# First up projection by Strassen in two groups of F tiles, with the modulation weights moved beside the down projections

## The reference, cut to what matters

```python
mod = (silu(c) @ w_ada + b_ada)            # 9 sections of 1024: shift, scale, gate for each of three blocks
h = modulate(rms_norm(x, g1), mod[0], mod[1])
x = x + 0.5 * mod[2] * ((silu(h @ Wg1) * (h @ Wu1)) @ Wout1)      # FFN 1, 2816 hidden
h = modulate(rms_norm(x, gmix), mod[3], mod[4])
x = x + mod[5] * (concat(pool_mixer(h @ Wa), gmlp_mixer(h @ Wzb)) @ Wmix_out)
h = modulate(rms_norm(x, g2), mod[6], mod[7])
x = x + 0.5 * mod[8] * ((silu(h @ Wg2) * (h @ Wu2)) @ Wout2)      # FFN 2, 2816 hidden
out = rms_norm(x, gfin)
```

## Time and profile before

| | |
|---|---|
| median of 3 runs | 884.86 us (884.81 to 887.31) |
| the profiled execution's own time | 886.71 us |
| its span in the profile | 885.0 us |
| TensorE busy | 859.1 us (97%) |
| VectorE busy | 584.4 us (66%) |
| ScalarE busy | 332.3 us (38%) |
| chain that ended last | PE 90%, DVE 5%, ACT 2% |
| mean granted clock of TensorE | 0.991 |
| moved by DMA | 134.46 MB, mean 152 GB/s |

### The profile page before, as it was taken

How to read it: one execution, slowest core, us unless ns; L and a number is a source line. 1 busy time by engine, 2 the same in 40 slices (tenths; PEclk the granted TensorE clock), 3 DMA queues, 4 the chain that set the end, 5 groups by cost and what they waited for, 6 DMA issues and landing times.

```text
span 885.0 us, 13666 instructions
## 1 busy us (share of the span) xinstructions
PE 859.1 (97%) x5290; PEld 743.5 (84%) x5290; DVE 584.4 (66%) x902; ACT 332.3 (38%) x434; POOL 36.0 (4%) x42
## 2 busy tenths in 40 slices
PE   4999999999999999999999999999999999999996
PEld 3778888888888888897887898899988899999886
DVE  4579777777776756538645469988633588885443
ACT  6232222222223221225424346665521256664323
POOL 0000000000000000000340000000000000100000
PEclk9899999999999999999999999999999999999998
DMA  9977666666656555434533322566343576562322
GB/s 268 289 215 234 191 191 191 192 194 191 194 179 204 160 172 166 146 108 108 142 96 96 94 73 72 139 173 171 85 130 93 118 181 165 148 168 83 99 66 96
DMA packets 219501, 134.46 MB, mean 152 GB/s; under 512 B 5577, under 2 KB 214589, under 8 KB 219453
## 3 DMA queue, kind: packets, MB, share of 16 engines
q1 hardware_dynamic: 216516, 128.52, 50.1%
q0 software_dynamic: 2880, 5.24, 3.7%
q10 hardware_dynamic: 56, 0.01, 0.0%
HBM read 126.41 MB, written 2.10 MB: 145 GB/s over the span
## 4 chain that ended last, share of the span: by engine, by line
PE 90%; DVE 5%; ACT 2%; SPq 1%; DMA 1%; issue 1%; ACTq 0%
PE ps L1569 22%; PE ps L1571 21%; PE ps L1570 21%; PE ps L1948 7%; PE ps L1944 7%; PE ps L1946 7%; PE ps L1826 1%; PE ps L1760 1%; DMA ada_first<-in_w_ada_dram 1%; PE ps L1827 1%; PE ps L1828 1%; DVE h_lo L1021 1%; DVE sw_lo_a L1447 1%; SPq L397 1%; DVE xs L1014 0%
## 5 line engine op out<-in xcount | busy, mean ns | idle before, releaser
L1569 PE MATMUL ps<-h_hi,w_split 128*128 128x512 f32 (+1 forms) x464 | 179.8, 388 | 5.5 <-DVE h_lo L1021 5.3
L1571 PE MATMUL ps<-h_hi,w_split 128*128 128x512 f32 (+1 forms) x464 | 180.0, 388 | 0.0
L1570 PE MATMUL ps<-h_lo,w_split 128*128 128x512 f32 (+1 forms) x464 | 178.9, 386 | 0.0
L968 DVE TENSOR_TENSOR w_split<-w_raw,w_split 128x2048 fp32r<-128x2048 f32 (+1 forms) x45 | 93.3, 2073 | 75.9 <-ACT w_split L610 75.9
L1569 PEld LDWEIGHTS ps<-h_hi,w_split 128*128 128x128 f32 x464 | 87.4, 188 | 26.9 <-issue 4.5
L610 ACT CAST w_split<-w_raw 128x2048 fp32r<-128x2048 f32 (+1 forms) x45 | 77.1, 1714 | 81.8 <-PE ps L1571 72.7
L1570 PEld LDWEIGHTS ps<-h_lo,w_split 128*128 128x128 f32 x464 | 87.6, 189 | 18.4
L1571 PEld LDWEIGHTS ps<-h_hi,w_split 128*128 128x128 f32 x464 | 87.6, 189 | 16.6
L1065 DVE SCALAR_TENSOR_TENSOR ada_acc<-ada_raw,c_act,ada_acc 128x256 f32<-128x256 f32 x196 | 95.1, 485 | 7.0
L1944 PE MATMUL ps<-sums_hi,sw_hi 128*128 128x256 f32 x320 | 89.3, 279 | 0.9 <-DVE sw_lo_a L1447 0.5
L1946 PE MATMUL ps<-sums_lo,sw_hi 128*128 128x256 f32 x320 | 89.6, 280 | 0.0
(11 more groups left out here) (186 smaller groups left out, 1533.2 us busy)
## 6 DMA issues: line engine op xcount, KB each, us to landing
ada_raw<-in_w_ada_dram SPq DMA_DIRECT2D x56, 512.0 KB, 3.6
sw_raw<-in_ffn_w_in_dram SPq DMA_DIRECT2D x100, 256.0 KB, 4.1
w_raw<-in_ffn_w_in_dram SPq DMA_DIRECT2D x47, 512.0 KB, 6.0
ada_first<-in_w_ada_dram SPq DMA_DIRECT2D x16, 512.0 KB, 7.4
w_raw<-in_ffn_w_out_dram SPq DMA_DIRECT2D x16, 384.0 KB, 4.0
w_raw<-in_w_mix_in_dram SPq DMA_DIRECT2D x12, 512.0 KB, 4.3
sw_raw<-in_ffn_w_out_dram SPq DMA_DIRECT2D x16, 384.0 KB, 4.1
w_raw<-in_ffn_w_out_dram SPq DMA_DIRECT2D x16, 320.0 KB, 3.3
```

The lines of the kernel that those rows point to most:

```text
L968: nc.vector.tensor_tensor(w_lo[s][:, 0:n], w_raw[s][:, 0:n], w_hi[s][:, 0:n].bitcast(F32), ALU.subtract).then_inc(lo_ready, 1)
L1569: nc.tensor.matmul(dst, w_h, a_h, start=start, stop=False)
L1570: nc.tensor.matmul(dst, w_h, a_l, start=False, stop=False)
L1571: return nc.tensor.matmul(dst, w_l, a_h, start=False, stop=stop)
```

## The change

FFN 1 takes the form of FFN 2. All helpers of FFN 2 get an index f and serve both.

- The first 8 tiles of F stay plain steps (`PLAIN = (8, 2)`), 14 go by Strassen: 3 in the first group of 11, then `down2(0, 0, m)` for 8 tiles m, then 11 more, then `down2(0, 1, m)`. a_hi and a_lo go; b_hi and b_lo serve both FFNs. The down products add to x in two parts, with the gate negated.
- The activation sums of FFN 1 are made beside the plain steps 2 and 3.
- The modulation unit is 512 columns wide, 14 units of two halves (four blocks of D, 1 MB each). A half is four multiply-adds of 512 elements; the second half of a unit also does the transpose and the sum. Eight halves run beside plain steps 0, 1, 1, 2, 4, 4, 5, 5 through ada_raw, which now holds one half; six beside each of FFN 1's two down groups and four beside the first down group of FFN 2 ("hosted": their data lie in the free end of the sw_raw slot of the down weights); four beside the mix.
- The modulation columns are taken over from the sums in five portions (`take_mod`, `TAKES`) in place of two.
- The mix's v weights have a buffer of their own (v_raw) and are requested within FFN 1's second down group.
- The order of SP's list, of VectorE's and of ScalarE's changes accordingly.

SP's list, the new part:

```diff
+            for j in range(2, PLAIN[0]):
+                load_pair(ffn1_w_in, j, j % 2, UP1 + j)
+                for part in {2: (0,), 3: (1, 2), 4: (3,), 5: (4,), 6: (5, 6), 7: (7,)}.get(j, ()):
+                    load_ada(part)
+            sp.wait_ge(ada_link, used(7))
+            for n in range(N0[0]):
+                load_up(0, n)
+            for m in range(KD):
+                load_down2(0, 0, m)
+            for n in range(N0[0], NS[0]):
+                load_up(0, n)
+            for m in range(KD):
+                load_down2(0, 1, m)
+                if m == KD - 4:
+                    sp.wait_ge(sw_used[0], pieces(0, up_item(0, NS[0] - 1) + 1))
+                    for kq in range(2):
+                        load_v(w_mix_in, kq)
+            sp.wait_ge(sw_lo_ready[0], pieces(0, down_item(0, 1, KD - 1) + 1))
+            sp.wait_ge(ada_link, used(19))
             for q in range(2):
+                load_two(w_mix_in, q * UNIT // 2, q, MIXIN + 2 + q)
+            load_ada(20)
+            sp.wait_ge(last_done, 2)
             sp.dma_start(ws_raw[:], w_spatial[0].rearrange("h t s -> t h s")).then_inc(ws_full, 16)
...
+            load_ada(21)
             for q in range(2, 4):
+                load_two(w_mix_in, q * UNIT // 2, q % 2, MIXIN + 2 + q)
             for q in range(KD // 2):
+                load_two(w_mix_out, q * UNIT // 2, q % 2, MIXOUT + q)
+                if q >= 2:
+                    load_ada(20 + q)
```

The two loaders of modulation halves:

```diff
+            def load_ada(part):
+                n = ADA_RAW.index(part)
                 for s in range(2):
+                    if n:
+                        sp.wait_ge(ada_link, used(ADA_RAW[n - 1], (s + 1) * KA // 2))
+                    k0 = part % 2 * KA + s * KA // 2
+                    sp.dma_start(ada_raw[:, s], w_ada_v[:, k0:k0 + KA // 2, ada_cols(part)])\
+                      .then_inc(ada_full[s], 16)
+            def load_down2(f, g, m):
+                i = down_item(f, g, m)
+                s = i % 2
+                sw_free(f, i, False)
...
+                if i in HOSTED[f]:
+                    part = HOSTED[f][i]
+                    k0 = part % 2 * KA
+                    host_free(f, i)
+                    sp.dma_start(host_view(s), w_ada_v[:, k0:k0 + KA, ada_cols(part)]).then_inc(host_full[f][s], 16)
```

VectorE and ScalarE beside FFN 1's plain steps:

```diff
+    ADA_PLAIN = {0: (0,), 1: (1, 2), 2: (3,), 4: (4, 5), 5: (6, 7)}
...
+            for j in range(PLAIN[0]):            # VectorE
+                plain_product(0, j)
+                if j == 0:
+                    for part in range(2):
+                        split_lo_part(2, part)
+                elif j + 2 < PLAIN[0]:
+                    split_lo(j + 2)
+                if j == 3:
+                    hsum_2(0)
+                    hsum_4(0)
+                    hsum_rest(0, 2)
+                    hsum_rest(0, 3)
+                plain_lo(0, j)
+                for part in ADA_PLAIN.get(j, ()):
+                    ada_own(part)
+                if j == 2:
+                    shift_difference(0)
+                    hsum_1(0)
+                    hsum_3(0)
+                    hsum_rest(0, 0)
+                    hsum_rest(0, 1)
+                elif j == PLAIN[0] - 2:
+                    add_blocks(0, 0)
+                    rest_up(0, 0, 0)
+                    rest_up(0, 0, 1)
+                elif j == PLAIN[0] - 1:
+                    rest_up(0, 0, 2)
+            up_group(0, 0)
...
+            for j in range(PLAIN[0]):            # ScalarE
+                plain_silu(0, j)
+                if j == 0:
+                    split_hi_part(2, 0)
+                    split_hi_part(2, 1)
+                elif j + 2 < PLAIN[0]:
+                    split_hi(j + 2)
+                if j == 2:
+                    plain_hi(0, j)
+                if j in (2, 3):
+                    for r in (2 * j - 4, 2 * j - 3):
+                        hsum_split(0, r)
+                if j != 2:
+                    plain_hi(0, j)
+                if j == PLAIN[0] - 2:
+                    for c in range(3):
+                        cast_up(0, 0, c)
+            first_group(0)
```

VectorE beside the down groups of FFN 1, and TensorE's list there:

```diff
+            for m in range(KD - 1):
...
+                rest_down(0, 1, m + 1)
...
+                if down_item(0, 1, m) in HOSTED[0]:
+                    ada_hosted(0, down_item(0, 1, m))
+                update_last(0, m)
+                add_squares(X_AT[0] + m + 1)
...
+            pe.wait_ge(prod_ready, 1)
+            plain(0, 2)
+            for j in range(3, PLAIN[0]):
+                pe.wait_ge(prod_ready, j - 1)
+                pair(j % 2, UP1 + j, (2 * (j % 2), 2 * (j % 2) + 1), h_hi, h_lo)
+            for n in range(N0[0]):
+                strassen(0, n)
+            sum_units(0)
+            for m in range(KD):
+                down2(0, 0, m)
+            for n in range(N0[0], NS[0]):
+                strassen(0, n)
+            for m in range(KD - 1):
+                if m == KD - 2:
+                    sum_units(1)
+                down2(0, 1, m)
```

More of the change, by code:

```diff
@@ L742, in copy_out @@
                 nc.scalar.copy(out_tok[:, :, bass.ds(m * P, P)], src).then_inc(out_copied, 1)
-            def down(base, x_count, sq_count, last):
-                nc.scalar.activation(dummy, ones[:, 0:1], ACT.Sqrt)
-                with act.Fori(0, KD - 1) as m:
-                    for s in range(2):
-                        split_hi(s, HALF, (m * 2 + (base + s + 2), m + (base // 2 + 1)))
-                    square(m, m + x_count, m + (sq_count + 1))
-                    if last:
-                        copy_out(m)
-                if not last:
-                    split_hi(0, FULL, base + 2 * KD)
-                act.wait_ge(sq_added, sq_count + KD)
@@ L761, in _ @@
+            first_group(0)
+            for n in range(N0[0], NS[0]):
+                up_slot(0, n)
+            for m in range(KD - 1):
+                cast_down(0, 1, m + 1)
+                if m == 0:
+                    product_hi(0, NS[0] - 1)
+                    nc.scalar.activation(dummy, ones[:, 0:1], ACT.Sqrt)
+                square(m, 0)
+            split_hi(MIXIN)
+            act.wait_ge(sq_added, KD)
             square_half(KD - 1, 0, 1, 0)
@@ L952, in _ @@
+            hsum_split(1, 0)
+            for c in range(3):
+                cast_up(1, 0, c)
+            hsum_split(1, 1)
+            hsum_split(1, 2)
+            plain_hi(1, 0)
+            plain_silu(1, 1)
+            first_group(1)
+            for n in range(N0[1], NS[1]):
+                up_slot(1, n)
+            for m in range(KD - 1):
+                cast_down(1, 1, m + 1)
+                if m == 0:
+                    product_hi(1, NS[1] - 1)
                     nc.scalar.activation(dummy, ones[:, 0:1], ACT.Sqrt)
-                square2(m)
+                square(m, 2)
@@ L1537, in _ @@
-            for n in range(N0):
-                up_slot(n)
+            split_lo_part(UP2 + 1, 0)
+            hsum_1(1)
+            split_lo_part(UP2 + 1, 1)
+            add_blocks(1, 0)
+            plain_product(1, 0)
+            hsum_rest(1, 0)
+            rest_up(1, 0, 0)
+            hsum_3(1)
+            hsum_2(1)
+            rest_up(1, 0, 1)
+            hsum_rest(1, 2)
+            hsum_rest(1, 1)
+            hsum_4(1)
+            rest_up(1, 0, 2)
+            plain_lo(1, 0)
+            hsum_rest(1, 3)
@@ new lines, in down2_half @@
+            def down2_half(m, half, between=None):
+                cols = HALVES[half]
+                hi, lo = (v.rearrange("p (k n) -> p k n", n=P) for v in (down_hi(m), down_lo(m)))
+                for k in range(GF):
+                    if between:
+                        between(k)
+                    ins = product(ps[:, LAST_BANK[half], cols], hi[:, k, :], lo[:, k, :], b_hi[:, k, cols],
+                                  b_lo[:, k, cols], k == 0, k == GF - 1)
+                ins.then_inc(last_done, 1)
@@ L2021, in _, with units_beside @@
-            for n in range(N0):
-                strassen(n)
+            pe.wait_ge(prod_ready, P_AT[1])
+            plain(1, 1)
+            def units_beside(k, n):
+                if k == GF // 2 + 1:
+                    pe.wait_ge(root_ready, 5)
+                    sum_units(n)
+            for n in range(N0[1]):
+                strassen(1, n)
             for m in range(KD):
-                down2(0, m)
-            for n in range(N0, NS):
-                strassen(n)
+                down2(1, 0, m, (lambda k, m=m: units_beside(k, 3 + m // 2)) if m in (1, 3) else None)
```

1352 lines of the change are left out of this document (606 added, 746 removed).

## The result

The changed kernel takes 909.84 us (median of 4 runs, 907.6 to 913.36), the kernel before on the same chip 884.84: a ratio of 1.028, 95% interval 1.0242 to 1.0318. So it is 25 us slower, where 20.8 were forecast (905.5 us, range 892 to 914). The profiled execution took 910.12 us, with a span of 908.4.

What follows compares the result with a forecast made beforehand. TensorE was taken to bound the kernel, VectorE next and full in the plain steps. FFN 1 saves 15.3 us and loses 30.4 (+15.1); mix +0.8, FFN 2 +1.4, clock +3.5: +20.8 on 884.86, forecast 905.5 us, range 892 to 914.

Steps and rivals of the forecast that it cites:

- the changes between up and down: Three switches between FFN 1's up and down parts: TensorE waits, 2.9 us including one short wait for the last chunk's weights.
- step 4: FFN 1 plain step: pair 4, requested behind parts 1 and 2, is split late, so the step starts 0.9 us late.
- step 5: FFN 1 plain step: VectorE's part 3 and activation sums delay the split, so the step starts 2.6 us late.
- step 7: FFN 1 plain step: pair 7 stands behind requests for parts 5 and 6, so the step starts 8.1 us late.
- first Strassen product: FFN 1 after step 7: its loads wait for all of part 7, so it starts 7.8 us late.
- third half product: First Strassen tile of FFN 1: late accumulation data delay VectorE and then ScalarE's copy, a 2.2 us wait.
- sixth chunk: FFN 1's second down group: chunk 5's weights land behind a hosted request and the v loads, 5.9 us late.
- sum of units 12: FFN 2: `sum_units(3)` needs parts 24 and 25 in one slot before block 6 of the second chunk, +1.4 us.
- the clock: After the 8.1, 7.8 and 5.9 us waits in FFN 1, TensorE's granted clock falls: +3.5 us.
- The clock staying up: Rival 1: no clock falls, since the waits lie in a dense stretch; +17.3 us, 902 us, chance 0.23.
- A queue slower or faster throughout: Rivals 2 and 3: DMA at 0.9 of the rate, 910 to 914 us, or 1.15 times, 897 to 900; chance 0.13 each.
- Rival 4: Plain steps: SP's list doesn't hold up the pairs, pair 7 requested by 103 us; 879.5 us, or 873; chance 0.08.

Runs made afterwards that it cites:

- e10: e8 with the v weights requested later, w_spatial ahead of half 20, and the sum of units 12 one block later: 875.27 us, ratio 0.988 to the kernel before.
- e8: Changed kernel with three buffers for the halves and the first Strassen tile requested early, pairs and halves in the change's own order: 880.62 us, ratio 0.9933.
- e9: e6 plus later v loads, earlier w_spatial, later sum of units 12, and three extra VectorE operations in each of plain steps 2 to 6: span 883.8 us.
- e4: Changed kernel with unused matmuls filling TensorE's waits at steps 4 and 7 and the first and third half products: 908.58 us, ratio 1.025.
- e1: Changed kernel with each pair of w_ffn1 requested ahead of the modulation halves it stood behind: 899.73 us, ratio 1.0142 to the kernel before.
- e3: Changed kernel with halves 0 to 7 in their own buffer, first Strassen loads not waiting for part 7: span from step 2's start 4.6 us shorter.
- e2: Changed kernel with the multiply-adds of the eight plain-step halves cut to 32 columns instead of 512: span 901.9 us, single execution.
- e6: Changed kernel with three buffers for the halves, the first Strassen tile requested early, and pairs ahead of halves as in e1: 881.9 us, ratio 0.9949.

## Why the prediction was right

**What is saved.** The period of a Strassen tile in FFN 1's second group, from VectorE's timeline, is 9.79 us (forecast 9.90):

```profile
263.30 0.69 DVE L1250 TENSOR_TENSOR ev<-ps,ev 128x512 f32<-128x512 f32 x1 [0.53 <-PE ps L1791]
273.09 0.69 DVE L1250 TENSOR_TENSOR ev<-ps,ev 128x512 f32<-128x512 f32 x1 [0.53 <-PE ps L1791]
```

That is not a better tile. In the traces the tiles have one of two periods, 9.89 or 9.79 us, one for a whole group at a time, and the kernel before has both: 9.89 in FFN 2's first group (the rows at 590.10 and 600.00 that I took in the earlier trace rows) and 9.79 in its second (721.28, 731.06, 740.85). The changed kernel has 9.79 in FFN 1's second group and 9.89 in FFN 2's second, e10 9.79 in both. A group of 11 tiles differs by 1.0 us between the two, which is more than several of the terms of the prediction; what sets the period was not found.

With the waits gone (e10) the first v product comes 13.0 us earlier than before (331.3 against 344.3). By my terms it would be 15.3 less 2.9 for the changes between up and down: 12.4. So the saving was there, as the earlier trace rows had it.

**VectorE's prices.** They held to the hundredth: multiply-add 0.751 us, transpose 0.712 (taken: 0.71), sum 0.686 (0.69), by the groups:

```profile
L1095 DVE SCALAR_TENSOR_TENSOR work<-ada_raw,c_act,work 128x512 f32<-128x512 f32 x42 | 31.5, 751 | 9.8 <-DMA ada_raw<-in_w_ada_dram 8.6
L1100 DVE STREAM_TRANSPOSE work<-work 128x512 f32<-128x512 f32 x14 | 10.0, 712 | 0.5
L1102 DVE TENSOR_REDUCE ada_part<-work 128x16 f32<-128x512 f32 x14 | 9.6, 686 | 0.5
```

The 66 us of work in the plain stretch were right too (63.2 busy in e8, and e9 shows that there is no room).

**The waits, term by term.** Forecast, then measured: step 4 0.9 and 3.4; step 5 2.6 and 1.0; step 7 8.1 and 8.8; first Strassen product 7.8 and 7.8; third half product 2.2 and 2.6; sixth chunk 5.9 and 2.8; w_spatial 0.8 and 0.9; sum of units 12 1.4 and 1.1; the three changes between up and down and the last chunk's weights 2.9 and 1.8 (0.4, 0.5, 0.7 and 0.2). The waits stand where they were forecast, and both large ones were right within 0.7 us: pair 7 came 7.4 us after its request (taken: 7.2), the first tile's loads 7.0 (6.8). Step 7 is right as a difference: pair 7 was requested 2.4 us later than forecast, and the step was due later too. Three terms were mis-sized.

Step 4: the cast came 10.0 us after the pair's request in place of 7.3. The queue wasn't slow, it carried 297 GB/s between the two. But it moved 4.1 MB from 60 us to the cast, and parts 1 and 2 and pair 4 are 3.1 MB:

```profile
60.00:77.75 17.75, 17.75 (x79) 14.55 (x79) 11.88 (x16) 1.22 (x2) 0.00 (x0) 1.00 0.80 233
```

So it was already carrying what was requested behind pair 4, and my assumption that requests are served one by one in the order of issue does not hold here. Step 5: 1.6 us less than forecast, since step 4's late start and its fall of the clock had put off the time at which it was due.

The sixth chunk: the prediction's own rate was not followed in its sum. 3.8 MB at 265 to 285 GB/s take 13.3 to 14.3 us and not the 15.9 from 371.6 to 387.5; by that rate the wait would have been 3.3 to 4.3 us. Measured, hosted half, v weights and chunk weights, 3.9 MB, landed 13.0 us after the first request:

```profile
378.10 0.37 SPq L523 DMA_DIRECT2D sw_raw<-in_w_ada_dram  x1
378.51 2.36 SPq L439 DMA_DIRECT2D v_raw<-in_w_mix_in_dram  x4
380.91 2.06 SPq L517 DMA_DIRECT2D sw_raw<-in_ffn_w_out_dram  x2
...
391.15 1.37 ACT L794 CAST sw_hi<-sw_raw 128x1408 fp32r<-128x1408 f32 x1 [3.02 <-DMA sw_raw<-in_ffn_w_out_dram]
```

Up to the second down group the changed kernel is 30.6 us behind e8 (296.9 against 266.3). Five waits are 23.6 of that. The four stretches at half speed make some 6: products of 512 columns start 0.43 us apart in place of 0.23 (127.57, 127.99, 128.42), for 2.9 to 3.4 us each. My terms for this part were 21.6 of waits and at most 3.5 for the clock, 5.5 short. The v loads, sized too large, gave 3.1 of it back, and behind FFN 2's second Strassen tile 1.0 more was lost than forecast, as much as the longer period there costs: so 25 came out and not 20.8. That the total is so near is in part luck, since the errors have both signs. (884.86 and 20.8 are 905.7; the 905.5 on record is a slip of 0.2.) Keeping the clock up (e4) gives 3.9 of the 6 us back; which wait takes up the rest was not tried singly.

**The clock.** Three falls were forecast, four came in FFN 1: after the waits of 3.4, 8.8 and 7.8 us, and after the 2.6 that followed shortly on the third. The wait of 2.8 before the sixth chunk brought none; I had counted one there. By the Trainium skill (TensorE: Matmul & The Clock Gate, "What's actually happening") the half rate is the default and an idle stretch brings it back: the trace agrees, at 0.50 in the window from 124 to 127 us. My 3.5 us stood for falls after the first Strassen product's wait and the sixth chunk's; the second did not come, and those that came cost some 6 where they stood.

**The rivals.** The clock staying up (902) is refuted by the windows. A queue slower or faster throughout is not borne out: the landings behind the two long waits took 7.4 and 7.0 us, near the 7.2 and 6.8 taken, while step 4's came later than forecast and the sixth chunk's earlier. Rival 4, the other side, was to be decided by whether pair 7 goes out by 103 or at 112.8. It went out at 115.2. In e8 it goes out at 94.9, the steps start in time, and the ratio of 0.9933 puts the median at 878.9, where rival 4 had 879.5; with the rest hidden it had 873, and e10's 0.988 gives 874. So rival 4 named the right switch. Its price is right by luck: its sum leaves out the sixth chunk (2.9 us in e8) and counts 4.8 for step 5 and the third half product, which don't wait in e8. As for the cause, the prediction had both parts of it, the one buffer and the order of the list; e1, e8 and e10 weigh them. The order matters only as long as one buffer holds one half, so that each request waits for VectorE.

## What to carry to other kernels

When an engine's list mixes loads for a bound engine (pairs for TensorE) with loads for a busy helper (halves for VectorE), every wait of the second kind is a wait of the first kind: look for the single buffer that makes a request wait for its consumer, and give it a second place in memory that is free at that time, before reordering the list (here the order alone gave 11 us from the common start, buffers and the first tile's early request 30). When a change saves on the bound engine and slows the kernel, take marks relative to a common start: here they put nearly all the loss into 100 us at the beginning, and the saving, untouched, behind it. An engine with 63 us of work in 66 is not yet a bottleneck, but only if nothing in its inputs has a round trip through its own progress.

## What the runs showed of the hardware

- A 3.4 us wait of TensorE at step 4, between dense stretches, was followed by a fall of the granted clock (0.65 over 81 to 85 us), and so was one of 2.48 us (e3). One of 2.78 us was not (1.00 over 394 to 398), nor one of 3.00 (e2, 1.00 over 387 to 391), while one of 2.97 (e6, 0.50 over 366 to 370) and one of 3.03 (e4, 0.52 over 391 to 394) were. Between 2.5 and 3.0 us the length of the wait alone does not tell whether the clock falls.
- Products that nobody reads kept the clock at 2.4 GHz through waits of 3 to 8 us in the plain steps (1.00 over 57 to 390 us of e4) and brought the first down group up to 3.9 us forward; the intervals of the two kernels' ratios overlap (1.0233 to 1.0267 and 1.0242 to 1.0318).
- The queue carried 338 GB/s over 6 us (388 to 394) and 353 over 4 us in e6, above the 285 of the earlier trace rows. Where the v loads came, it carried more: 401 over 4 us (381 to 385). The Trainium skill (DMA: Bandwidth & Descriptors, "Where 436 GB/s comes from") has some 358 GB/s as the limit of a core's share of the memory; the window at 381, in a program that runs on one core, is above it.
- The queue did not carry requests one at a time: when pair 4 was cast, 4.1 MB had moved since 60 us, 1 MB more than pair 4 and all requested ahead of it.
- A Strassen tile took 9.79 or 9.89 us, the same for a whole group, and the same code had one in one execution and the other in another (FFN 2's second group: 9.79 before, 9.89 in the changed kernel, 9.79 in e10).
- The same VectorE operation of 512 elements took 0.418 us into SBUF and 0.685 into PSUM (e9, the groups below). The Trainium skill (VectorE: DVE Perf Modes, "Why PSUM operands drop a tier") has it that an operand in PSUM takes away the fast mode that such an operation has in SBUF; the two rows agree. Here the operand in PSUM is the one that is written.

```profile
381.00:385.00 4.00, 4.00 (x19) 3.30 (x18) 3.89 (x5) 0.00 (x0) 0.00 (x0) 1.00 1.05 401
388.00:394.00 6.00, 3.46 (x16) 2.50 (x14) 2.14 (x2) 1.50 (x2) 0.00 (x0) 1.00 1.12 338
...
81.00:85.00 4.00, 2.87 (x7) 2.32 (x8) 3.89 (x6) 0.00 (x0) 0.00 (x0) 0.65 0.23 58
```

```profile
L1428 DVE TENSOR_SCALAR ps<-h_lo 128x512 f32<-128x512 f32 x10 | 6.4, 685 | 0.0
...
L1428 DVE TENSOR_SCALAR work<-h_lo 128x512 f32<-128x512 f32 x5 | 2.1, 418 | 0.0
```
